# Attention steps of one item put together in TensorE's order, instead of singly between products

## The reference, cut to what matters

```
sc = einsum('bkgqd,bskd->bkgqs', q, k) * scale      # logits, a block of 128 queries against up to 512 keys
p  = softmax(sc)                                    # D: softmax(sc0) - lam * softmax(sc1)
o  = einsum('bkgqs,bskd->bqkgd', p, v)              # output
mix = o * silu(g)                                   # gate; D: an RMS norm of o first
```

## Time and profile before

| | |
|---|---|
| median of 3 runs | 1554.2 us (1551.07 to 1554.65) |
| the profiled execution's own time | 1553.3 us |
| its span in the trace | 1551.2 us |
| PE busy | 1418.2 us (91%) |
| DVE, ACT, POOL busy | 903.9, 682.7, 367.7 us (58%, 44%, 24%) |
| mean granted TensorE clock | 0.974 |
| DMA | 131.72 MB, mean 85 GB/s |

### The profile page before, as it was taken

The page is one execution under the profiler, slowest core; times in us unless marked ns, Lnnn a source line. Parts: engine busy times, 40 slices in busy tenths (PEclk is TensorE's granted clock), DMA queues, the critical chain, the costliest instruction groups (busy, mean ns, idle before and its releaser), DMA issues.

```text
span 1551.2 us, 21240 instructions
## 1 busy us (share of the span) xinstructions
PE 1418.2 (91%) x8026; PEld 1092.2 (70%) x8026; DVE 903.9 (58%) x1705; ACT 682.7 (44%) x1478; POOL 367.7 (24%) x265
## 2 busy tenths in 40 slices
PE   6799998999989999999998799997999799998997
PEld 5666685777987576767788666665777656665776
DVE  3646437557672553484576575568655466558655
ACT  2445444455233553445552444335443444335443
POOL 1224122245231321222451111410001112310011
PEclk9999999999999999999999799998999899998999
DMA  6542211225343121211263323511313322511211
GB/s 213 139 103 68 76 61 41 62 61 204 109 138 80 29 82 56 82 40 51 67 224 90 88 55 69 116 55 49 95 62 96 82 65 58 116 55 48 96 62 55
DMA packets 191448, 131.72 MB, mean 85 GB/s; under 512 B 91764, under 2 KB 181492, under 8 KB 191348
## 3 DMA queue, kind: packets, MB, share of 16 engines
q1 hardware_dynamic: 179302, 110.19, 26.0%
q10 hardware_dynamic: 12046, 20.19, 3.9%
HBM read 118.03 MB, written 12.32 MB: 84 GB/s over the span
## 4 chain that ended last, share of the span: by engine, by line
PE 69%; DVE 18%; ACT 8%; issue 3%; DMA 1%; ACTq 1%; POOL 0%; DVEq 0%; SPq 0%; POOLq 0%
PE pb L1390 18%; PE pb L1391 16%; PE pb L1392 16%; PE pb L1468 6%; PE pb L1412 5%; PE pb L1446 4%; ACT prob L1524 2%; ACT wh L1542 2%; ACT tmp L1524 1%; DVE wl L1851 1%; DVE small L2116 1%; DVE xl L1858 1%; PE pb L1430 1%; DVE scr L2138 1%; DMA wr<-w_in 1%
## 5 line engine op out<-in xcount | busy, mean ns | idle before, releaser
L2283 POOL TENSOR_TENSOR wl<-wr,wh 128x512 fp32r<-128x512 f32 x170 | 237.2, 1395 | 896.8 <-ACT wh L1542 893.0
L1390 PE MATMUL pb<-xh,wl 128*128 128x512 f32 (+1 forms) x832 | 352.2, 423 | 29.2 <-DVE xl L1858 21.7
L1391 PE MATMUL pb<-xl,wh 128*128 128x512 f32 (+1 forms) x832 | 322.6, 388 | 0.0
L1392 PE MATMUL pb<-xh,wh 128*128 128x512 f32 (+1 forms) x832 | 322.0, 387 | 0.0
L1851 DVE TENSOR_TENSOR wl<-wr,wh 128x512 fp32r<-128x512 f32 x200 | 164.0, 821 | 164.6 <-ACT wh L1542 164.3
L1390 PEld LDWEIGHTS pb<-xh,wl 128*128 128x128 f32 x832 | 162.4, 195 | 110.0 <-issue 60.1
L1542 ACT CAST wh<-wr 128x512 fp32r<-128x512 f32 x370 | 211.0, 603 | 58.8 <-PE pb L1392 31.2
L1392 PEld LDWEIGHTS pb<-xh,wh 128*128 128x128 f32 x832 | 162.4, 195 | 31.9
L1391 PEld LDWEIGHTS pb<-xl,wh 128*128 128x128 f32 x832 | 163.3, 196 | 24.2 <-issue 3.8
L1524 ACT ACTIVATE prob<-prob,small 128x512 f32<-128x512 f32 (+3 forms) x128 | 76.2, 597 | 147.2 <-DVE small L2093 147.1
L1446 PE MATMUL pb<-cst,prob 128*128 128x128 f32 x768 | 118.9, 276 | 23.9 <-ACT prob L1524 13.1
(11 more groups left out here) (196 smaller groups left out, 2448.6 us busy)
## 6 DMA issues: line engine op xcount, KB each, us to landing
wr<-w_in SPq DMA_DIRECT2D x40, 1024.0 KB, 5.4
wr<-w_in SPq DMA_DIRECT2D x48, 256.0 KB, 4.5
wr<-w_out SPq DMA_DIRECT2D x10, 1024.0 KB, 6.1
wr<-w_branch SPq DMA_DIRECT2D x48, 128.0 KB, 2.3
x<-prob SPq DMA_DIRECT2D x12, 512.0 KB, 2.6
wr<-w_out SPq DMA_DIRECT2D x48, 128.0 KB, 3.0
wr<-w_mem_kv SPq DMA_DIRECT2D x4, 1024.0 KB, 8.0
prob<-x ACTq DMA_DIRECT2D x2, 2048.0 KB, 10.3
```

What stands on the lines that cost most here:

```text
L1390: e.matmul(ps, ll, rh, start=start, stop=False)
L1391: e.matmul(ps, lh, rl, start=False, stop=False)
L1392: t = e.matmul(ps, lh, rh, start=False, stop=stop)
L2283: t = e.tensor_tensor(wl[:, j % 2, c0:c1], wr[:, j % 2, c0:c1], wh[:, j % 2, c0:c1].bitcast(F32), ALU.subtract)
```

## The change

For each item the new `attention` puts the turns of the item before, the outputs whose copies were asked for an item earlier, and the front of this item, without a yield between them. Then it yields a negative time (`MIDS`: 1500 ns for sb, 4000 for D, 3000 for the others), at which `alongside` may go on regardless of the attention's share, puts `mid`, and yields the time of the exponentials (`EXPS`; D 7500 instead of 7000). The output of an item's pair of blocks is put one item later than before. The list `nothing` of D's later steps loses its first, empty entry. The planned costs change a little: a piece of 512 columns from 693 to 678 ns, one of 256 from 346 to 360, logits of 512 keys from 860 to 1040.

```diff
-EXPS = {"sb": 7000, "D": 7000}
+EXPS = {"sb": 7000, "D": 7500}
+MIDS = {"sb": 1500, "D": 4000}
...
-        return len(s["ks"]) * 3 * n * 0.451
+        return len(s["ks"]) * 3 * (14 + 0.414 * n)
...
-        return 128 * (hi - lo) * (3.36 if s["br"] in ("mla", "fox") else 1.68)
+        n = 128 * (hi - lo)
+        return 3.35 * n if s["br"] == "fox" else (200 + 1.64 * n) * (2 if s["br"] == "mla" else 1)
...
-        def back(c, i, es, ready, mid):
-            yield ready
+        def turns_of(c, i, es):
             for half in range(2):
                 if i % 2 == 0:
                     tt[half] = TT.take()
                 b = AT.take()
                 put("turn", l=l, br=br, c=c, i=i, half=half, b=b, e=es[half], t=tt[half])
                 give(b, es[half])
-                if half == 0:
-                    yield 0
-                    mid()
-            copied = now() + COPIES
             advance()
             if i == 3 and br != "sb":
-                yield 0
                 b = AT.take()
                 put("rturn", l=l, br=br, c=c, b=b, rt=rt[c], u=us[0])
                 give(b, rt[c])
             if i % 2:
-                yield copied
+                owed.append((c, i, tt[0], tt[1]))
+
+        def outputs(which):
+            for c, i, t0, t1 in which:
+                owed.remove((c, i, t0, t1))
                 if i == 1:
                     ob[c] = OB.take()
-                put("pv", l=l, br=br, c=c, ih=i // 2, b=ob[c], t=(tt[0], tt[1]))
-                give(tt[0], tt[1])
+                put("pv", l=l, br=br, c=c, ih=i // 2, b=ob[c], t=(t0, t1))
+                give(t0, t1)
...
-                es, mid, after = front(l, br, c, i, sm.get(c), rt)
+                ripe = list(owed)
+                if before:
+                    turns_of(*before)
+                outputs(ripe)
+                es, mid = front(l, br, c, i, sm.get(c), rt)
                 ready = now() + EXPS.get(br, 4000)
-                yield 0
-                if late:
-                    late()
-                if before:
-                    yield from back(*before, mid)
-                else:
-                    mid()
-                before, late = (c, i, es, ready), after
-        if late:
-            late()
-        yield from back(*before, nothing)
+                yield -(now() + MIDS.get(br, 3000))
+                mid()
+                yield ready
+                before = c, i, es
+        ripe = list(owed)
+        turns_of(*before)
+        outputs(ripe)
+        yield now() + COPIES
+        outputs(list(owed))
         while later:
             yield now() + 2500
             advance()
...
-            if ready is not None and now() >= ready and (f - f0) * total_m >= m * span:
+            if ready is not None and now() >= abs(ready) and (ready < 0 or (f - f0) * total_m >= m * span):
...
-            return [nothing, scaled, corrected, gated]
+                return [scaled, corrected, gated]
```

More of the change, by code:

```diff
@@ L251, in cost_of @@
     if k == "pv":
-        return sum(1.68 * (hi - lo) for _, lo, hi in output_spans(s["br"], s["ih"]))
+        return sum(1.64 * (hi - lo) for _, lo, hi in output_spans(s["br"], s["ih"]))
     if k in ("rturn", "vturn", "feat"):
         return 436
-    if k in ("dqk", "squares", "rope1", "rope2", "qsquares", "dsquares"):
+    if k == "dqk":
+        return 1036
+    if k in ("squares", "rope1", "rope2", "qsquares", "dsquares"):
         return 860
@@ L423, in attention @@
     def attention(l, br, front, finish):
-        later, sm, rt, tt, ob = [], {}, {}, {}, {}
+        later, sm, rt, tt, ob, owed = [], {}, {}, {}, {}, []
         def advance():
@@ L462, in back @@
                         later.append(rest)
-            yield 0
         us, finish = finish
-        before, late = None, None
+        before = None
         for c in range(2):
@@ L470, in attention @@
             for i in range(4):
-                es, mid, after = front(l, br, c, i, sm.get(c), rt)
-                ready = now() + EXPS.get(br, 4000)
-                yield 0
-                if late:
-                    late()
-                if before:
-                    yield from back(*before, mid)
-                else:
-                    mid()
-                before, late = (c, i, es, ready), after
-        if late:
-            late()
-        yield from back(*before, nothing)
+                ripe = list(owed)
[3 more added lines that the diff above has]
+                es, mid = front(l, br, c, i, sm.get(c), rt)
+                ready = now() + EXPS.get(br, 4000)
+                yield -(now() + MIDS.get(br, 3000))
[7 more added lines that the diff above has]
+        outputs(list(owed))
         while later:
@@ L499, in softmax_front @@
         give(*b)
-        return es, (lambda: recip(br, c, es, sm, rt)) if i == 3 else nothing, None
+        return es, (lambda: recip(br, c, es, sm, rt)) if i == 3 else nothing
     def diff_front(l, br, c, i, sm, rt):
@@ L511, in mix @@
                 recip(br, c, es, sm, rt)
-        return es, mix, None
+        return es, mix
     def stick_front(l, br, c, i, sm, rt):
@@ L521, in sticks @@
             give(*ta)
-        return es, sticks, None
+        return es, sticks
     def out_gated(u, yc):
@@ L553, in alongside @@
         while ready is not None:
-            if now() >= ready or f > LEAD:
+            if now() >= abs(ready) or f > LEAD:
                 ready = step(tail)
@@ L1000, in plan, with out_diff, f, scaled @@
         first = {}
[L1002 to L1021, removed]
-            return [nothing, scaled, corrected, gated]
+        def out_diff(u):
+            def f(l, br, c, ob):
+                put("dout", l=l, c=c, b=ob)
+                if c:
+                    put("accload", l=l)
+                ta = TA.take()
+                put("dgate", l=l, c=c, u=u, ta=ta)
+                held = []
+                def scaled():
+                    held.append(GR[0].take())
+                    put("dsquares", l=l, c=c, b=held[0], ta=ta)
+                def corrected():
+                    tn = TN.take()
+                    put("dnewton", l=l, c=c, b=held[0], ta=ta, tn=tn)
+                    give(held[0], tn)
+                def gated():
+                    put("dsplit", l=l, c=c, ta=ta)
+                    give(ta)
+                return [scaled, corrected, gated]
+            return f
         def part(i, m, k, b=None):
@@ L1035, in plan @@
             if br == "D":
-                att = attention(l, br, diff_front, ([u], out_diff))
+                att = attention(l, br, diff_front, ([u], out_diff(u)))
             else:
```

## The result

The changed kernel takes 1612.1 us (median; 1609.9 to 1613.0) beside 1554.4 for the kernel before in the same comparison. The ratio is 1.037, with a 95% interval from 1.036 to 1.039: slower by 58 us. The direction of the prediction and its main mechanism, the overrun, held; the size was twice what its sum gave (+28.8), and the time lies at the upper end of the range.

What follows compares the result with a forecast made beforehand. PE's own work plus its idle time was taken to bound the kernel (PE busy 91%). Overruns of 78.4 us, less 44.6 of removed waits and 5 of grouping, gave +28.8: forecast 1582 us, range 1545 to 1612.

Steps and rivals of the forecast that it cites:

- the overrun: Attention items left when a branch's products run out, in D, sb and C: 39.2 us a layer, 78.4 for two layers.
- One item at a time: All branches: each needs 8 intervals of products; D's items 5 to 7 and sb's 6 and 7 stand bare.
- Latency of D's bare items: D's end in C's stretch: PE idle 2.1 us for item 5, 9.5 for items 6 and 7, 7.4 at the end; 19.0.
- The clock: PE at 1.2 GHz after gaps: 4, 2 and 1 us a layer for D, sb, C; bounds 0 and 13, 5, 2.
- the third rival: Clock stays low throughout the bare stretches: 13 + 5 + 2 instead of 4 + 2 + 1, 1608 to 1625 us; chance 0.12.
- 2 x (11.3 - 6.0): sb, two layers: overrun of 11.3 us a layer (9.3 idle, 2 clock) less 6.0 of removed waits.
- C's was 9.8: C's end, two layers: overrun of 4.9 us a layer, 3.9 idle and 1 for the clock.
- 2 x (23.0 - 13.3): D, two layers: overrun of 23.0 us a layer less 13.3 removed (10.3 waits - 2 bank waits + 5 clock).
- Waits removed: PE's waits on the attention lines: 44.6 us saved, 2 x 19.3 in D and sb plus 6 elsewhere.
- Grouping: Turns, outputs and logits put together save PE returns from and entries to outputs: 5 us, bounds 2 and 10.
- Rival 2: Grouping saves 0.2 us on each of about 190 visits, 38 us instead of 5: 1549 us, near no change; chance 0.12.
- rival 1: Cheap overrun, 20 us a layer (D 12, sb 6, C 2), no clock loss: faster, 1544 us; chance 0.16.

Runs made afterwards that it cites:

- sb alone: Only sb takes the new loop, every other branch keeps the loop of the kernel before: 1578.6 us, ratio 1.014 to the kernel before.
- D alone: Only D takes the new loop, every other branch keeps the loop of the kernel before, with the new costs: 1578.7 us, ratio 1.015.

## Why the prediction was right in kind and wrong in size

- **One item at a time: right, and the cause.** Which items stand bare came out as counted: D's items 5 to 7 and its end, sb's 6 and 7 and its last copies. With two items under way the loss is gone (0.999).
- **Latency of D's bare items: right in sum, partly by luck.** 19.9 us a layer measured against 19.0. Within it item 5 waited 5.3 instead of 2.1. Its maxima started 1.1 us late, behind the scaling of the pair before it (two operations on DVE and one on ACT, about 0.7 each), which the sum had only at the end. Its mix then started 4.65 us after the maxima, instead of 2.40 for item 6: a weight split (L1857 at 1121.70) stood ahead of it in DVE's queue and waited for ACT's copy, which the sum did not have. Items 6 and 7 waited 3.8 instead of 4.5, and the end 7.0 instead of 7.4.
- **The clock: the step that failed.** The sum took 4, 2 and 1 us a layer for it and credited 5 a layer at D for gaps removed, a net of 2 x (7 - 5) = 4 us. Measured are 26.1 us of longer busy time for the same matmuls, and by the stretches at 1.2 GHz the clock's own part is 33. The credit was right: in the stretch of the earlier trace rows PE worked at 1.2 GHz for 8.8 us before, worth 4.4, and not at all after. The cost was not. In layer 0, D's end has 21.5 + 5.4 = 26.9 us of work at 1.2 GHz, which cost 13.4 instead of 4, just over the bound of 13; sb's end has 14.9, which cost 7.5 instead of 2, over the bound of 5. The middle value stood for a clock that comes back between the gaps. It came back while PE stood, and was low again for the work. With PE kept at work in the waits the kernel's own matmuls are busy for 35.2 us less. The 7 us between 33 and 26.1 are not explained; the 5 of grouping may be among them. This is the mechanism of the third rival (1608 to 1625), given 0.12. The Trainium skill ("TensorE: Matmul & The Clock Gate", section "HAM oscillation — how this bites in real kernels") says that a kernel with waits between short bursts starts every one of them cold; the turns at 2.21, 2.23 and 2.24 us agree.
- **sb: the branch that was mis-sized.** Its net term was 2 x (11.3 - 6.0) = 10.6 us; alone it measured 22. C's was 9.8 against 4.4 alone. sb's waits were as long as predicted (8.8 a layer, 2.52, 1.32, 3.03, 1.14 and 0.77, against 9.3), so the miss is the clock around them and a longer wait of the product behind (2.66 and 3.07 us for DVE's L2019, 1.57 before). The trace of sb alone bears this out: PE is busy for 1433.5 us, 15.3 more than before, where the sum had 4 for sb's clock, and idle for 11.1 more, where it had 6.6.
- **D: near in sum, by luck.** Its net term was 2 x (23.0 - 13.3) = 19.4 us against 23 alone. The sum had 21.4 more of idle time and 2 less for the clock; the trace of D alone has 13.3 more of idle time and 9.0 more of busy time. Such differences of single traces are good to some 3 us.
- **Waits removed: they went, and others came.** The 3.6 and 3.1 of the earlier trace rows are gone. In their place are two groups that no term of the sum had: the turn of the reciprocals waits for them, 9.8 us in 8, and the squares of a correction 8.5 instead of 4.2 in 6. Both are put right behind what computes them. They stand in the kernel with only the five other branches changed too, which is 3.4 us faster all the same; the sum had up to 11 for grouping and for waits there. The idle time, forecast at 28.8 - 4 = 24.8 more, came to 33.9; these 14.1 of new waits (9.8, and 4.3 more at the squares) are larger than the 9.1 between.
- **Grouping: nearly nothing.** 5 us were predicted, with 2 as the lower bound. No kernel shows it apart; with the grouping and two items the time is that of before, with new waits in it and 5.9 us less of busy time. Rival 2 (38 us) is excluded by that run, and rival 1, a cheap overrun, by D's 23 and sb's 22 us alone.
- **Open:** about 8 of the 58 us, which the branches give only together. Each interval reaches some 3 us to either side, so part of it may be measurement. That D gave back only 10.8 us when its loop was undone in the changed kernel may come from the delay of 7.5 us for about 7; the rest is not explained, nor that sb gave back 32 there and cost 22 alone.

## What to carry to other kernels

When the latency of an item is longer than the products it may claim, keep two items under way before asking how the pieces are grouped: visits to attention cost PE next to nothing here, and the item left over at a branch's end costs 4 to 5 us of waiting each. Price a bare end twice, once for its waits and once for its work at half clock: here several gaps of 3 to 5 us with 4 to 7 us between them left 21.5 of 23.5 us of PE's work at 1.2 GHz. Take the latency of a chain from where it will run, with what the other engines have in their queues there: from the logits to the first turn it was 3.8 us bare and 6.0 to 8.4 beside products, where the mix also stood behind weight splits.

## What the hardware showed that was not expected

- The low clock met the work and missed the gaps. In 1124 to 1162.7 us the mean clock was 0.68, with gaps of 3.76, 3.84, 2.80 and 4.16 us and 4 to 7 us from the end of one gap to the start of the next, but 21.5 of the 23.5 us of work were at 1.2 GHz and the clock stood at 1.00 in 1130.56 to 1133.98, where PE did nothing. The mean clock of a stretch alone does not give the cost; the busy time inside its parts at 0.50 does. The single gaps of the earlier trace rows, with up to 3.6 us, had left 8.8 of 55.2 us of work at 1.2 GHz.
- Work without use paid: 204 matmuls that hold nothing of use took 47.4 us of PE, 34.9 of them in time that had been idle; the kernel's own matmuls took 35.2 us less, and the kernel came down by 21.1.
